# A recurrence chain and its group norm: both heads in one PSUM bank, the norm by halves of the tokens, Sqrt and reciprocal in place of Ln and Exp

## The chip, the cores and the metric

The kernel runs on one core of one Trainium2 chip. Its time is the device time of one execution, in microseconds. Engine names in the rows: PE is TensorE (PEld its weight loads), DVE is VectorE, ACT is ScalarE, POOL is GpSimd, SP is SyncE, which issues the DMAs.

## The reference

256 tokens pass two blocks of width 2048 in float32. The first block has two layers of windowed attention beside a gated convolution. The second has an RWKV-7 mixer of 16 heads (64 wide) beside latent attention, an output projection and a gated feed-forward part. The change is mostly in what follows the RWKV scan:

```python
y = rwkv7_scan(r, decay, k, v, -kk, kk * a)
mu = jnp.mean(y, axis=-1, keepdims=True)                 # over the 64 of a head
var = jnp.mean(jnp.square(y - mu), axis=-1, keepdims=True)
y = ((y - mu) * lax.rsqrt(var + GN_EPS)).reshape(bsz, s, c) * gn_w + gn_b
bonus = jnp.sum(r * k * r_k, axis=-1, keepdims=True) * v
out = (y + bonus.reshape(bsz, s, c)) * g                 # g = sigmoid(h_g) @ g2
x = x + jnp.concatenate([out, y_mla], axis=-1) @ w_out
```

## The kernel before

Weights come in 385 MB of "units", each 128 x 2048 floats, that pass a ring of four places. SyncE loads unit u + 4 when TensorE has finished unit u (`sp_unit`); ScalarE copies it rounded (`act_split`, L229), VectorE or GpSimd subtracts to get the low part (L234, L241), and TensorE multiplies: per block k of the operand one matmul of 128x512 with the high part (L259; the last one L262) and one of 128x256 with the low part (L260), in `both_halves`. Every engine runs its list of stages in the order in which they are written; only semaphores tie the engines together.

**The front** (`phase_front`, once for each of two layers) goes through positions m = 0 to 45, a unit each. Beside the units it does the attention of head pair h: scores on TensorE, softmax, `transposes(h)` at m = 12 + 4h into PSUM banks 2 and 3, `probs(h)` on ScalarE (L585, the copy of them into SBUF), and `values(h)` on TensorE (L885) at m = 13 + 4h. On ScalarE `probs(h)` stands at m = 13 + 4h, behind the split of that position. From m = 36 on, ScalarE has a `gate(m)` (L563) at the end of each position that waits for VectorE.

**Within** (`phase_within`): 16 items (8 pairs of heads, two halves of the tokens). In it TensorE computes for chunks of 32 tokens what the recurrence needs.

**The chain** (`phase_chain`): 8 chunks, c = 1 to 7 in sequence. TensorE computes "next" (L2072, the next state, 16 products of 64x64 tiles) and "y" (L2074, 16 products), one tile for each of the two heads of a pair: rows 0 to 63 and rows 64 to 127. Head 0 writes bank 2 (or 4), head 1 bank 3 (or 5). VectorE adds step_n to each half (L2092) and y to kk (L2099). Between chunks TensorE does something else: `early_products` of the first units of the output projection out2 (which need only the attention half of the operand) and `gates(x)` (L2056 with 128 rows and L2057 with 32 rows), which ScalarE (L2043) and VectorE (L2105) read.

**The norm** (`phase_norm`): `head_sums` (L1713) of y over the heads, VectorE subtracts the mean (L2161), ScalarE squares (L2145), head sums of the squares, ScalarE Ln (L2148) and Exp with -0.5 (L2151), VectorE multiplies and adds (L2165, L2172, L2173), ScalarE and VectorE write the high (L2154) and low (L2169) part of the operand, two blocks at a time. Here a "half" is four of the eight blocks of channels with all tokens.

**out2** (`phase_residual` with `early`): units 0 to 3 were loaded and split long before, and blocks 8 to 15 of each are already multiplied; blocks 0 to 7 of unit 0 wait for the norm's operand pair by pair. `keep_running` (L298) issues matmuls of 128x512 whose result nobody reads ("fillers"): 8 at the end of within, 4 and 2 in the norm, 9 between the blocks of unit 0. Two more pairs of them lie in the last item of within and stay.

`link(...)` makes VectorE wait for its own previous instruction.

## Time and profile before

| | |
|---|---|
| Time, median of 3 runs | 2209.92 us (2209.63 to 2210.14) |
| The profiled execution: its time, its span | 2208.75 us, 2207.0 us |
| Mean granted TensorE clock | 0.998 |
| TensorE busy | 2169.7 us, 98% of the span |
| VectorE, ScalarE, GpSimd busy | 1713.8, 1071.9 and 544.9 us |
| Moved by DMA | 384.73 MB, 174 GB/s |

The span is from the first to the last record of the profiled execution; its time is what the same execution took by the measure of the runs, 1.75 us more. A granted clock of 1.00 is the full one (2.4 GHz), 0.50 the half (1.2 GHz). Busy times are those of an engine's instructions; matmuls overlap in the records, so that a busy TensorE needn't be at its peak.

### The profile page before, as it was taken

What the parts mean: (1) busy time and instruction counts of PE and PEld (TensorE: products, weight loads), DVE (VectorE), ACT (ScalarE), POOL (GpSimd) and SP (SyncE); (2) the same over time, 40 slices, a digit from 0 to 9 for tenths busy, and PEclk for the clock granted to TensorE, in tenths of its full rate; (3) what the DMA queues carried; (4) which work ended last, traced back from release to release, by engine and by line L of the source; (5) the groups of instructions that cost most, each with busy time, mean ns of one, the idle gap of its engine ahead of it and who ended that gap; (6) DMA issues with size and microseconds to landing.
All of it is one profiled execution on the core that took longest, in us unless ns stands there. A gap on an engine that the chain in (4) does not pass through costs nothing.

```text
span 2207.0 us, 38356 instructions
## 1 busy us (share of the span) xinstructions
PE 2169.7 (98%) x14358; PEld 1893.7 (86%) x14358; DVE 1713.8 (78%) x2889; ACT 1071.9 (49%) x1435; POOL 544.9 (25%) x225
## 2 busy tenths in 40 slices
PE   7999999999999999999999999999999999999997
PEld 6888888888888888899999787888888888888886
DVE  7799678886999588788888666888888874447887
ACT  5555464444555654556545533444444443333454
POOL 4776731018776620210003302100000000000001
PEclk9999999999999999999999999999999999999999
DMA  7554445555555455554455200555555555555554
GB/s 256 186 180 174 159 173 190 190 181 202 183 175 181 153 182 182 189 193 166 156 180 181 82 22 26 204 189 184 183 187 189 190 190 185 184 185 189 190 212 169
DMA packets 69030, 384.73 MB, mean 174 GB/s; under 512 B 15088, under 2 KB 22768, under 8 KB 23984
## 3 DMA queue, kind: packets, MB, share of 16 engines
q1 hardware_dynamic: 68912, 383.09, 48.9%
q8 instruction: 82, 1.34, 0.3%
q14 instruction: 36, 0.29, 0.0%
HBM read 379.89 MB, written 3.18 MB: 174 GB/s over the span
## 4 chain that ended last, share of the span: by engine, by line
PE 68%; POOL 14%; issue 11%; DVE 4%; DMA 1%; ACT 1%; SPq 0%; POOLq 0%; DVEq 0%; ACTq 0%
PE ps L259 33%; PE ps L260 18%; POOL low L241 14%; PE ps L247 3%; PE ps L248 3%; PE ps L249 3%; PE ps L262 2%; DMA raw<-weights_dram 1%; DVE low L234 1%; PE ps L1861 1%; PE ps L1913 0%; PE ps L1905 0%; PE ps L1713 0%; PE ps L1850 0%; DMA inst<-chunk_mats_dram 0%
## 5 line engine op out<-in xcount | busy, mean ns | idle before, releaser
L259 PE MATMUL ps<-opA,whi 128*128 128x512 f32 x2460 | 871.2, 394 | 0.0
L260 PE MATMUL ps<-opA,low 128*128 128x256 f32 x2624 | 706.7, 279 | 0.2 <-DVE opA L983 0.2
L229 ACT ACTIVATE whi<-raw 128x2048 fp32r<-128x2048 f32 x346 | 660.2, 1909 | 78.5 <-DMA raw<-weights_dram 77.2
L234 DVE TENSOR_TENSOR low<-raw,whi 128x2048 fp32r<-128x2048 f32 x252 | 583.9, 2317 | 67.0 <-ACT whi L229 51.1
L259 PEld LDWEIGHTS ps<-opA,whi 128*128 128x128 f32 x2460 | 461.0, 187 | 106.0 <-issue 3.0
L241 POOL TENSOR_TENSOR low<-raw,whi 128x2048 fp32r<-128x2048 f32 x95 | 436.4, 4610 | 409.0 <-ACT whi L229 382.7
L259 PE MATMUL ps<-opB,whi 128*128 128x512 f32 x1380 | 494.1, 398 | 14.0 <-DVE opB L418 11.6
L260 PEld LDWEIGHTS ps<-opA,low 128*128 128x128 f32 x2624 | 492.0, 187 | 14.6 <-DVE opA L983 0.5
L260 PE MATMUL ps<-opB,low 128*128 128x256 f32 x1472 | 397.5, 280 | 0.0
L259 PEld LDWEIGHTS ps<-opB,whi 128*128 128x128 f32 x1380 | 259.7, 188 | 77.5 <-DVE low L412 10.4
L268 ACT ACTIVATE crossed<-ps 128x256 f32<-128x256 f32 x168 | 64.5, 384 | 492.0 <-PE ps L262 491.8
L260 PEld LDWEIGHTS ps<-opB,low 128*128 128x128 f32 x1472 | 277.3, 188 | 7.7
L723 DVE SCALAR_TENSOR_TENSOR ps<-a_in,par,ps 128x256 f32<-128x256 f32 x464 | 226.8, 489 | 14.6
L259 PE MATMUL ps<-act_hl,whi 128*128 128x512 f32 x672 | 237.2, 394 | 0.3
L1126 POOL MEMSET ssq<- 128x256 f32 (+1 forms) x4 | 1.5, 367 | 805.0 <-DVE t L975 677.2
L260 PE MATMUL ps<-act_hl,low 128*128 128x256 f32 x704 | 191.4, 279 | 0.0
L247 PE MATMUL ps<-opB,whi 128*128 128x256 f32 x560 | 161.2, 288 | 0.2 <-DVE ps L1435 0.2
L249 PE MATMUL ps<-opB,low 128*128 128x256 f32 x560 | 158.0, 282 | 0.0
L248 PE MATMUL ps<-opB,whi 128*128 128x256 f32 x560 | 157.7, 282 | 0.0
L259 PEld LDWEIGHTS ps<-act_hl,whi 128*128 128x128 f32 x672 | 125.9, 187 | 30.9 <-issue 2.2
L260 PEld LDWEIGHTS ps<-act_hl,low 128*128 128x128 f32 x704 | 132.0, 187 | 2.6
L1130 POOL TENSOR_TENSOR ssq<-ssq,sq 128x256 f32<-128x256 f32 (+1 forms) x63 | 60.6, 962 | 249.2 <-ACT sq L1043 184.3
(393 smaller groups left out, 2608.7 us busy)
## 6 DMA issues: line engine op xcount, KB each, us to landing
raw<-weights_dram SPq DMA_DIRECT2D x350, 1024.0 KB, 4.8
bias_t<-table_dram SPq DMA_DIRECT2D x16, 384.0 KB, 5.9
hT<-xT_dram SPq DMA_DIRECT2D x4, 512.0 KB, 9.0
out_dram<-hT SPq DMA_DIRECT2D x3, 512.0 KB, 2.8
lora_g<-lora_dram SPq DMA_DIRECT2D x1, 1024.0 KB, 5.1
p_in<-pT_dram SPq DMA_DIRECT2D x2, 256.0 KB, 5.1
lora_wa<-lora_dram SPq DMA_DIRECT2D x1, 512.0 KB, 6.4
chunk_mats_dram<-compact SPq DMA_DIRECT2D x4, 128.0 KB, 3.3
```

What stands on the lines that cost most here:

```text
L229: act.activation(whi[:, v % RING, :], raw[:, v % RING, :], ACT.Copy).then_inc(hi_done.sem, 1)
L234: v_.tensor_tensor(wlo(v % RING, 0, width), raw[:, v % RING, 0:width], whi[:, v % RING, 0:width].bitcast(F32), ALU.subtract).then_inc(lo_d ...
L241: pool.tensor_tensor(wlo(v % RING), raw[:, v % RING, :], whi[:, v % RING, :].bitcast(F32), ALU.subtract).then_inc(lo_done.sem, 1)
L247: pe.matmul(dst, whi[:, s, w0:w0 + P], op[:, k, 0:T], start=start, stop=False)
L248: pe.matmul(dst, whi[:, s, w0:w0 + P], op[:, k, T:2 * T], start=False, stop=False)
L249: return pe.matmul(dst, wlo(s, w0, w0 + P), op[:, k, 0:T], start=False, stop=stop)
L259: pe.matmul(*cross, start=start, stop=False)
L260: mm = pe.matmul(ps[:, b, 0:T], wlo(s, w0, w0 + P), op[:, k, 0:T], start=False, stop=False)
L262: mm = pe.matmul(*cross, start=False, stop=True)
L268: act.activation(crossed[:, b, :], ps[:, b if bank is None else bank, T:2 * T], ACT.Copy).then_inc(read.sem, 1)
L723: link(v.scalar_tensor_tensor(y, taps, w, y, ALU.mult, ALU.add))
L1130: pool.tensor_tensor(total, total, part, ALU.add).then_inc(summed.sem, 1)
```

## The change

Five things, in the words of the code:

- **Front.** `probs(h)` for h = 0 to 6 stands on ScalarE at m = 12 + 4h, after the copy of that position's half and before `gate(m)`, instead of behind the split of the next position. `probs(7)` stays.
- **Chain, heads in one bank.** Both heads' "next" go to bank 2, both "y" to bank 4; VectorE adds all 128 partitions in one instruction.
- **Gates in one tile shape.** The second product of a gate takes all 128 rows (the added rows of the weights are zero); gates come after chunks 1, 2, 3 and 5.
- **Norm by halves of the tokens.** A "half" is now 128 tokens of all eight blocks. The first half's tokens are finished after chunk 3: its head sums (kk after chunk 4, squares after chunk 6), its centring, squares, Sqrt and first multiplication move into the chain. Ln and Exp give way to Sqrt on ScalarE and a reciprocal on VectorE.
- **Order and fillers.** Early products: unit 0 before the chain, unit 1 after chunk 7, units 2 and 3 in the norm, blocks 8 to 11 of all four behind the last head sums. ScalarE's copy and GpSimd's subtraction of y_mla's second half move into within; scm, held and the bank of unit 0 move. The fillers at the end of within, in the norm and in unit 0 are left out.

The core of the diff (context and smaller lines left out):

```diff
-if x == 0 and 1 <= h <= PAIRS:
+if x == 0 and h == PAIRS:
...
+if x == 3 and 0 <= h < PAIRS - 1:
+    probs(h)
...
-pe_unit(pe, u0, j, i, op, kb=KB // 2, start=False, bank=early[m], need=0, ready=ready if opening else None, wide=True,
-        filler=(lambda k: (3 if k in (2, 4, 6) else 0, 2)) if opening else None)
+pe_unit(pe, u0, j, i, op, kb=KB // 2, start=False, bank=early[m], need=0, ready=ready if opening else None, wide=True)
...
-def head_sums(pe, src, half):
-    for n in range(4 * half, 4 * half + 4):
-        mm = pe.matmul(ps[:, 2 + n // 2, (n % 2) * T:(n % 2) * T + T], head_ones[:, :], src[:, n, :], start=True, stop=True)
+def half(x, h):
+    return x[:, :, h * P:h * P + P]
+def head_sums(pe, src, h):
+    for b in range(2):
+        mm = pe.matmul(ps[:, 5 + b, :], head_ones[:, :], src[:, 4 * b:4 * b + 4, h * P:h * P + P], start=True, stop=True)
-sums = ps[:, 2:6, :].rearrange("p b (c t) -> p (b c) t", c=2)
+sums = ps[:, 5:7, :].rearrange("p b (c t) -> p (b c) t", c=4)
+sq_, rstd = uS[:, 0:8, :], uS[:, 16:24, :]
+def centred(v, h):
+    v.wait_ge(*rw_p(2 * h + 1))
+    v.scalar_tensor_tensor(half(kk, h), sums, -1.0 / DH, half(kk, h), ALU.mult, ALU.add).then_inc(no["centred"].sem, 1)
...
-scm = place("scm", [P, 2, 2, 3, P], at=second + 24 * T)
-def phase_within(u_next):
+scm = place("scm", [P, 2, 2, 3, P], at=word_rows)
+def phase_within(u_next, op):
...
+pool.wait_ge(*ch["mla_hi"](1))
+pool.tensor_tensor(op[:, 12:16, T:2 * T], y_mla[:, 4:8, :], op[:, 12:16, 0:T].bitcast(F32), ALU.subtract).then_inc(ch["mla_lo"].sem, 1)
...
-keep_running(pe, u_next, 8, 2)
...
+if n == 4:
+    act.wait_ge(*ml["stored"](MLA_H))
+    act.activation(op[:, 12:16, 0:T], y_mla[:, 4:8, :], ACT.Copy).then_inc(ch["mla_hi"].sem, 1)
...
-held = place("held", [P, 4, DH], at=word_rows)
+held = place("held", [P, 4, DH], at=word_rows + 6 * T)
...
-early_bank = (6, 7, 0, 1)
+early_bank = (3, 7, 0, 1)
-        both_halves(pe, u, early_bank[n], k * P, op, k, k == (8 if n >= 2 else 12), False)
+        both_halves(pe, u, early_bank[n], k * P, op, k, k == 12, False)
...
-pool.wait_ge(*ch["state"](1))
-pool.wait_ge(*ch["mla_hi"](1))
-pool.tensor_tensor(op[:, 12:16, T:2 * T], y_mla[:, 4:8, :], op[:, 12:16, 0:T].bitcast(F32), ALU.subtract).then_inc(ch["mla_lo"].sem, 1)
...
-act.wait_ge(*wi["mn"](4 * RW_B))
-act.activation(op[:, 12:16, 0:T], y_mla[:, 4:8, :], ACT.Copy).then_inc(ch["mla_hi"].sem, 1)
+act.activation(small[:, 3:4], small[:, 7:8], ACT.Sqrt)
-        act.wait_ge(*ch["state"](NCH - 1))
-        act.activation(op[:, 8:12, 0:T], y_mla[:, 0:4, :], ACT.Copy).then_inc(ch["mla_hi"].sem, 1)
+        act.wait_ge(*no["centred"](1))
+        act.activation(half(sq_, 0), half(kk, 0), ACT.Square).then_inc(no["sq"].sem, 1)
+act.wait_ge(*ch["state"](NCH - 1))
+act.activation(op[:, 8:12, 0:T], y_mla[:, 0:4, :], ACT.Copy).then_inc(ch["mla_hi"].sem, 1)
+act.wait_ge(*rw_p(2))
+act.activation(half(rstd, 0), sums, ACT.Sqrt, scale=1.0 / DH, bias=small[:, 6:7]).then_inc(no["dev"].sem, 1)
...
-        mm = pe.matmul(dst, lora_g[0:32, 1, n * P:n * P + P], g1[0:32, :], start=False, stop=True)
+        mm = pe.matmul(dst, lora_g[:, 1, n * P:n * P + P], g1, start=False, stop=True)
+pe.wait_ge(*ch["mla_lo"](1))
+early_products(pe, u_next, 0, range(12, 16), op)
...
-                        mm = pe.matmul(ps[r, 2 + h, pair * DH:pair * DH + DH], step_m[r, pair, c // 4, c % 4, :], s, start=True, stop=True)
+                        mm = pe.matmul(ps[r, 2, pair * DH:pair * DH + DH], step_m[r, pair, c // 4, c % 4, :], s, start=True, stop=True)
-                        mm = pe.matmul(ps[r, 4 + h, pair * CH:pair * CH + CH], s, r_[r, pair, c * CH:c * CH + CH], start=True, stop=True)
+                        mm = pe.matmul(ps[r, 4, pair * CH:pair * CH + CH], s, r_[r, pair, c * CH:c * CH + CH], start=True, stop=True)
-        if c == 1:
-            pe.wait_ge(*ch["mla_lo"](1))
-        if c <= 2:
-            early_products(pe, u_next, c - 1, range(12, 16), op)
-        elif c <= 6:
-            gates(c - 3)
+        if c <= 3:
+            gates(c - 1)
+        elif c == 4:
+            pe.wait_ge(*ch["y_read"](3))
+            head_sums(pe, kk, 0)
+        elif c == 5:
+            gates(3)
+        elif c == 6:
+            pe.wait_ge(*no["sq"](1))
+            head_sums(pe, sq_, 0)
+        else:
+            early_products(pe, u_next, 1, range(12, 16), op)
+    link = dve_chain.start(v)
-            for h in range(2):
-                r = slice(DH * h, DH * h + DH)
-                ins = v.tensor_tensor(state[r, (c + 1) % 2, :, :], ps[r, 2 + h, :].rearrange("p (b d) -> p b d", b=RW_B),
-                                      step_n[r, :, c // 4, c % 4, :], ALU.add)
-            ins.then_inc(ch["state"].sem, 1)
+            v.tensor_tensor(state[:, (c + 1) % 2, :, :], ps[:, 2, :].rearrange("p (b d) -> p b d", b=RW_B),
+                            step_n[:, :, c // 4, c % 4, :], ALU.add).then_inc(ch["state"].sem, 1)
-        for h in range(2):
-            r = slice(DH * h, DH * h + DH)
-            dst = kk[r, :, c * CH:c * CH + CH]
-            ins = v.tensor_tensor(dst, ps[r, 4 + h, 0:T].rearrange("p (b t) -> p b t", b=RW_B), dst, ALU.add)
-        ins.then_inc(ch["y_read"].sem, 1)
-        if c >= 4:
-            x = c - 4
+        dst = kk[:, :, c * CH:c * CH + CH]
+        v.tensor_tensor(dst, ps[:, 4, 0:T].rearrange("p (b t) -> p b t", b=RW_B), dst, ALU.add).then_inc(ch["y_read"].sem, 1)
+        if c in (2, 3, 4, 6):
+            x = min(c - 2, 3)
+        if c == 4:
+            centred(v, 0)
+        if c == 6:
+            v.wait_ge(*no["centred"](1))
+            link(v.tensor_tensor(half(gate_w, 0), half(gate_w, 0), half(kk, 0), ALU.mult))
+    link.end()
-y, sq_, rstd = kk, uS[:, 0:8, :], uS[:, 16:24, :]
-def half(x, h):
-    return x[:, 4 * h:4 * h + 4, :]
-    keep_running(pe, u_next, 4, 2)
-    for h in range(2):
-        head_sums(pe, y, h)
-    pe.wait_ge(*ch["mla_lo"](2))
-    early_products(pe, u_next, 0, range(8, 10), op)
-    for h in range(2):
-        pe.wait_ge(*no["sq"](h + 1))
-        head_sums(pe, sq_, h)
-    early_products(pe, u_next, 0, range(10, 12), op)
-    early_products(pe, u_next, 1, range(8, 12), op)
+    pe.wait_ge(*no["dev"](1))
+    head_sums(pe, kk, 1)
-        early_products(pe, u_next, n, range(8, 16), op)
-    pe.wait_ge(*no["ln"](2))
-    keep_running(pe, u_next, 2, 2)
+        early_products(pe, u_next, n, range(12, 16), op)
+    pe.wait_ge(*no["sq"](2))
+    head_sums(pe, sq_, 1)
+    pe.wait_ge(*ch["mla_lo"](2))
+    for n in range(4):
+        early_products(pe, u_next, n, range(8, 12), op)
-    act.activation(small[:, 3:4], small[:, 7:8], ACT.Ln)
-    for h in range(2):
-        act.wait_ge(*no["centred"](h + 1))
-        act.activation(half(sq_, h), half(y, h), ACT.Square).then_inc(no["sq"].sem, 1)
-    for h in range(2):
-        act.wait_ge(*rw_p(h + 3))
-        act.activation(half(rstd, h), half(sums, h), ACT.Ln, scale=1.0 / DH, bias=small[:, 6:7]).then_inc(no["ln"].sem, 1)
-    for h in range(2):
-        act.wait_ge(*no["ln"](h + 1))
-        act.activation(half(rstd, h), half(rstd, h), ACT.Exp, scale=-0.5).then_inc(no["rstd"].sem, 1)
+    act.wait_ge(*no["centred"](2))
+    act.activation(half(sq_, 1), half(kk, 1), ACT.Square).then_inc(no["sq"].sem, 1)
+    act.wait_ge(*rw_p(4))
+    act.activation(half(rstd, 1), sums, ACT.Sqrt, scale=1.0 / DH, bias=small[:, 6:7]).then_inc(no["dev"].sem, 1)
...
-for h in range(2):
-    v.wait_ge(*rw_p(h + 1))
-    v.scalar_tensor_tensor(half(y, h), half(sums, h), -1.0 / DH, half(y, h), ALU.mult, ALU.add).then_inc(no["centred"].sem, 1)
-v.wait_ge(*ch["g_read"](RW_B // 2))
+v.wait_ge(*no["dev"](1))
+link(v.reciprocal(half(rstd, 0), half(rstd, 0)))
+centred(v, 1)
+link(v.tensor_tensor(half(gate_w, 0), half(gate_w, 0), half(rstd, 0), ALU.mult))
+link(v.tensor_tensor(half(gate_w, 0), half(gate_w, 0), half(bonus, 0), ALU.add))
-for h in range(2):
-    link(v.tensor_tensor(half(gate_w, h), half(y, h), half(gate_w, h), ALU.mult))
+link(v.tensor_tensor(half(gate_w, 1), half(gate_w, 1), half(kk, 1), ALU.mult))
+v.wait_ge(*no["dev"](2))
+link(v.reciprocal(half(rstd, 1), half(rstd, 1)))
-    v.wait_ge(*no["rstd"](n // 2 + 1))
-    link(v.tensor_tensor(pair_of(gate_w, n), pair_of(gate_w, n), pair_of(rstd, n), ALU.mult))
-    v.tensor_tensor(pair_of(gate_w, n), pair_of(gate_w, n), pair_of(bonus, n), ALU.add).then_inc(no["gated"].sem, 1)
+    last = half(pair_of(gate_w, n), 1)
+    link(v.tensor_tensor(last, last, half(pair_of(rstd, n), 1), ALU.mult))
+    v.tensor_tensor(last, last, half(pair_of(bonus, n), 1), ALU.add).then_inc(no["gated"].sem, 1)
...
```

## Rows read from the trace of the kernel before

**Rows 1.** Busy by stretch: length; PE, PEld, DVE, ACT, POOL; granted clock; DMA.
```profile
1351.00:1369.00 18.00, 18.00 (x113) 15.28 (x110) 11.06 (x15) 10.96 (x13) 1.24 (x1) 1.00 0.00 1
```

**Rows 2.** The chain of work that ended last, steps 6, 7 and norm: start, us, what.
```profile
1346.20 1.08 PE ps L2072 x32
1347.28 0.91 PE ps L2074 x32
1348.18 0.63 PE ps L2056 x2
1348.81 0.62 PE ps L2057 x2
...
1350.69 1.05 PE ps L2074 x32
...
1352.87 3.55 PE ps L1713 x16
```

**Rows 3.** Timeline of VectorE, chain and norm: start, us, engine, line, operation, [idle before].
```profile
1325.63 1.39 DVE L2092 TENSOR_TENSOR state<-ps,step_n 64x512 f32<-64x512 f32 x2 [1.25 <-PE ps L2072]
...
1351.79 0.86 DVE L2099 TENSOR_TENSOR kk<-ps,kk 64x256 f32<-64x256 f32 x2 [1.28 <-PE ps L2074]
...
1357.79 2.49 DVE L2165 TENSOR_TENSOR gate_w<-kk,gate_w 128x1024 f32<-128x1024 f32 x2
...
1370.99 1.47 DVE L2169 TENSOR_TENSOR opB<-gate_w,opB 128x512 fp32r<-128x512 f32 x2
```

**Rows 4.** Timeline of TensorE: first chain step, ends of units 0 and 1, start of unit 4.
```profile
1324.44 1.15 PE L2072 MATMUL ps<-state,step_m 64*64 64x64 f32 x32 [0.19 <-DVE state L2086]
...
1373.69 0.39 PE L262 MATMUL ps<-opB,whi 128*128 128x512 f32 x1
...
1376.50 0.40 PE L262 MATMUL ps<-opB,whi 128*128 128x512 f32 x1
...
1383.94 0.47 PE L259 MATMUL ps<-opB,whi 128*128 128x512 f32 x1 [1.44 <-DVE small L1093]
```

**Rows 5.** Timeline of ScalarE: within stage (the first row) and norm.
```profile
1314.93 0.28 ACT L1964 ACTIVATE tokA<-ps 128x128 f32<-128x128 f32 x1 [2.04 <-PE ps L1905]
...
1355.99 1.06 ACT L2145 ACTIVATE uS<-kk 128x1024 f32<-128x1024 f32 x1 [2.91 <-DVE kk L2161]
...
1360.86 1.12 ACT L2148 ACTIVATE uS<-ps,small 128x1024 f32<-128x1024 f32 x1 [0.62 <-PE ps L1713]
```

**Rows 6.** Reciprocals, grouped by line and shape: count, busy us, mean ns, idle before.
```profile
L448 DVE RECIPROCAL rs<-sq 128x256 f32<-128x256 f32 x1 | 1.8, 1753 | 0.1
L1809 DVE RECIPROCAL st<-st 128x2 f32<-128x2 f32 x8 | 1.3, 158 | 0.1
```

**Rows 7.** Waits of TensorE over the whole kernel: us in total, times, longest.
```profile
PE ps L885 <- ACT probsT L585: 2.8, 2, 1.4
```

**Rows 8.** Timeline of ScalarE around position 37 of the first front.
```profile
249.75 0.39 ACT L563 ACTIVATE ps<-az 128x256 f32<-128x256 f32 x1 [4.58 <-DVE bz_s L711]
...
251.88 1.00 ACT L585 ACTIVATE probsT<-ps 128x1024 f32<-128x1024 f32 x1
```

**Rows 9.** Timeline of TensorE at the same place.
```profile
244.77 0.71 PE L876 MATMUL ps<-ident,sm 128*128 128x128 f32 x5
...
252.93 1.08 PE L885 MATMUL ps<-probsT,v_tok 128*64 128x256 f32 x8 [1.41 <-ACT probsT L585]
```

**Rows 10.** Busy time and granted clock at the kernel's end (columns as in rows 1).
```profile
2194.00:2196.00 2.00, 0.52 (x3) 0.27 (x2) 1.20 (x4) 0.66 (x2) 0.00 (x0) 1.00 0.00 0
2196.00:2198.00 2.00, 0.43 (x2) 0.03 (x1) 0.95 (x1) 0.47 (x1) 0.00 (x0) 0.81 0.00 0
```

**Rows 11.** Timeline of TensorE, early matmuls of the kernel.
```profile
11.17 0.63 PE L259 MATMUL ps<-opB,whi 128*128 128x512 f32 x1
...
11.81 0.63 PE L259 MATMUL ps<-opB,whi 128*128 128x512 f32 x1
...
17.55 0.44 PE L259 MATMUL ps<-opB,whi 128*128 128x512 f32 x1
```

More of the change, by code:

```diff
@@ L495, in reuse_front_semaphores @@
                                    (ch, ("state", "next", "y", "y_read", "mla_hi", "mla_lo", "g", "g_read", "shift")),
-                                   (no, ("lora", "centred", "sq", "var", "ln", "rstd", "gated", "hi", "lo"))):
+                                   (no, ("lora", "centred", "sq", "dev", "gated", "hi", "lo"))):
                 for n in names:
@@ L2300, in program @@
         u += IN2_UNITS + UP_UNITS
-        following = phase_within(u)
+        following = phase_within(u, opnd[1])
         stages += [phase_mla(u, following), following]
```

## The prediction, made before the changed kernel was run

> **What bounds the kernel now.** I read the busy time by stretches first: in the norm stage TensorE is busy for all 18 us, at the full clock, and VectorE for 11 of them [rows 1]. But part of that TensorE work are fillers, so the chain of waits comes next. In a chain step with gates it runs over TensorE alone: the "next" products 1.08 us, the "y" products 0.91, then four gate products of 0.62 to 0.63 us each, 4.5 us a step [rows 2]. VectorE's timeline shows the other loop: two state additions 1.39 us, two y additions 0.86 [rows 3]. The norm that follows is a dependence chain over three engines. TensorE's timeline shows where it ends: unit 0 of out2 is done at 1374.08, and unit 4 starts at 1383.94, 9.9 us later, after 1.44 us of waiting [rows 4]. Unit 4's weights are only loaded when unit 0 is done, while units 1 to 3 take 8.4 us (2.81 each [rows 4]): so the end of unit 0 sets the end of the kernel, and some 1.4 us of TensorE's work in units 1 to 3 is free. In the front I read the list of waits, then both timelines: values() waits twice for probsT, 1.4 us each time [rows 7].
>
> **The front.** The wait is at position 37, one in each layer. probs(6) stands behind gate(36), which ScalarE gets to at 249.75 only (it waits for VectorE), and behind the split at 250.07; it runs at 251.88, and TensorE resumes at 252.93 with 1.41 us idle. The transposes that probs(6) reads began at 244.77 [rows 8, 9]. Moved ahead of gate(36), it runs near 246 and the wait is gone. Behind it: the gate and the split stay where VectorE puts them, and I see nothing that the chain would meet later that isn't itself released by TensorE. At the six earlier positions the copy now delays a weight split by about 1.1 us; GpSimd, whose subtraction uses that split, is still busy with the previous one then, so I take 0. Term: 2 x 1.41 = -2.8 us. Bounds: 0 and -2.8.
>
> **End of the within stage.** The 8 fillers give way to four early products of unit 0 (4 x 0.35 = 1.4 us). Both lie beside the last evictions; "next" still waits for VectorE's first state copy, so its start at 1324.44 stays. ScalarE's copy of y_mla (128x1024, about 1.06 us as Square over as many elements) moves to item 4; ScalarE has some 2 us idle in each item [rows 5]. Without that cover it would cost 1 us. GpSimd's subtraction goes with it; GpSimd has nothing to do there. 0.
>
> **The chain.** Two halves of 64 partitions become one instruction of 128: state 1.39 to 0.70 us, y 0.86 to 0.43 [rows 3]. The loop over VectorE is then 1.15 + 0.7 + 0.45, under TensorE's step, so this is worth only 0.43 us, at the last y. The gates: each of their products takes two matmul records of 256 columns. The head sums of the same size run at 3.55/16 = 0.22 to 0.23 us a record, 0.46 a product, against 0.62 and 0.63 here, where products with 128 rows and with 32 alternate [rows 2]. I take the difference, 0.16 us, for the change of shape. In one shape only the first pays it: 0.63 + 3 x 0.465 = 2.02 us instead of 2.5. (If it is something else, the gates stay at 2.5: four steps x 0.48 = +1.9 us.) The two head sums that move in are 16 records' worth halved, 1.86 + 0.16 = 2.02 us too. Steps 1 to 6 each hold such a filler: 6 x (1.08 + 0.91 + 2.02) = 24.06 us, then y 1.05 and the addition 0.43. From 1324.44 that ends at 1349.98; before it was 1351.79 + 0.86 = 1352.65. Term -2.7. The waits that come in (gate weights read, shift, centred, square) I placed on this grid; each is satisfied 0.5 us or more before TensorE asks. Of ScalarE's work there, two splits, the Sqrt table load and the first gate read end near 1330, and VectorE needs that read at 1331.
>
> Heads in one bank could cost. The two halves are row tiles 0 to 63 and 64 to 127, which today write two banks and overlap: 32 records of 64 columns in 1.08 us are 0.034 each, while 256 columns of a full tile at 0.23 are 0.058 for 64 [rows 2]. Without the overlap, "next" takes 32 x 0.058 = 1.86 us, +0.78 in six steps = +4.7 us; "y", with 32 columns, stays where it is. Every pair of row tiles in this kernel writes two banks, so no row here shows the case. The Trainium skill (TensorEngine Tiling, "Gotcha 1: PSUM Pressure") says that different row tiles cannot access the same PSUM bank simultaneously; by it the 4.7 us would be paid. I take 0, because the two halves also differ in their output partitions, and keep it as a rival.
>
> **The norm.** Ln and Exp on ScalarE go; Sqrt and VectorE's reciprocal over 128x1024, twice, come. The rows for reciprocals: 128x2 0.158 us, 128x256 1.753 us, so 1.595/254 = 6.28 ns an element [rows 6]; a tensor_tensor over 128x1024 at 1.25 us is some 1.2 ns an element [rows 3]. Over 1024 elements: 0.158 + 1022 x 0.00628 = 6.58 us each. Bounds: from below 1.75, if the cost went by instruction (the 2-element row speaks against that); from above 4 x 1.753 = 7.0. The Trainium skill (VectorE: DVE Perf Modes, "First, the fixed hardware budget") gives the iterative divide a repeat count of 8; at eight passes of about 1.04 ns an element, an estimate, each would be 8.5 us and the sum 3.9 us more. The rows decide for 6.58.
>
> VectorE from 1350.0: reciprocal(0) 6.58 (its Sqrt, as long as today's Ln, 1.12 us [rows 5], ends at 1349.6), centred(1) 1.25, times rstd, plus bonus, times kk: 3 x 1.25 [rows 3]. Meanwhile centred(1) releases Square 1.06, head sums 1.86 and Sqrt 1.12 [rows 5], 4.2 us with hand-overs, so dev(2) comes at 1362.15, 0.5 us after VectorE is free. Then reciprocal(1) to 1368.8, and the tail (eight 128x256 operations at 0.43, and low parts at 0.7 which wait for ScalarE's high parts) 6.0 us: the last low part ends at 1374.85, against 1372.46 before [rows 3]. The 9 + 4 + 2 fillers go. From the last low part to unit 0's end it was 1374.08 - 1372.46 = 1.62 us, three fillers among them, so about 0.95 now (k 6, k 7 at 0.35 and the drain). Unit 0 ends at 1375.8 instead of 1374.08: +1.7 us for chain and norm together, the chain's -2.7, the norm's +5.1 and -0.7 for the fillers.
>
> **The clock.** TensorE now has two gaps: about 1355.8 to 1359.0, and 1366.6 to 1371.2, after which pairs of products come one per 1.3 us. What gaps do shows at the end of the kernel: with 0.52 us of work in 2 us and then 0.43, the granted clock, 1.00 until 2196, has a mean of 0.81 over 2196 to 2198: at half from near 2197.2 on, some 3 us after dense work ended [rows 10]. The kernel's first products take 0.64 us per k (11.17 to 11.81), where 0.35 (2.81/8) is normal; at 17.55 the same matmul takes 0.44 us instead of 0.63 [rows 4, 11], so the slow pace lasted up to 6 us. I expect the fall to 1.2 GHz in the second gap: unit 0's last pair 1.3 us later, and of the slow start in units 1 to 3 (up to 5 k x 0.29 = 1.5 us) most is covered by the free 1.4: +0.3. Term +1.6.
>
> **Sum.** -2.8 + 1.7 + 1.6 = +0.5 us. The profiled execution took 2208.75 us (span 2207.0), so 2209.3 on it; the median of the runs is 2209.92, 1.2 higher: **2210.4 us**.
>
> **Rivals.**
> - The clock holds in both gaps: 2210.4 - 1.6 = 2208.8. For it: TensorE is not quite empty in between. Chance 0.22.
> - It falls in the first gap too: the head sums of the second half take 1.9 us more, on the path: 2212.3. The gap is 3.2 us, at the length that the kernel's end shows. 0.14.
> - The front's wait moves elsewhere (the y_sq sums at 39, where TensorE already waits now and then): 2213.2. 0.10.
> - Slower: row tiles in one bank don't overlap, +4.7: 2215.1. It decides (past 2214.3) once "next" takes over 1.73 us, 0.65 more in six steps. For it: the kernel gives every other pair of row tiles two banks; against it: here their output partitions differ. 0.10. The gates' shape not being the cause (+1.9: 2212.3): 0.05.
> - The change does more than this: reciprocals by instruction, not by element. Then centred, Square, sums and Sqrt bind, and unit 0 ends 8 us earlier: 2202. 0.03.
> - My forecast, a fall in the second gap only: 0.36, with its own range 2208 to 2212.
>
> **Range and chances.** 0.2% is 4.4 us, about what a measurement of this kernel can tell from no change. Faster than 2205.5 lies only the cheap reciprocal and an error in my grid: 0.06. Slower than 2214.3: the bank rival, or two of the +2 cases together: 0.14. Same: 0.80. The range 2206 to 2214.5 leaves out the bank rival and the cheap reciprocal.
>
> **What would show it.** Reciprocals of 6.6 us at the two new lines; "next" at 1.1 us; steps of 4.0 us; no wait of values() at position 37; granted clock under 1.00 in the stretch behind the norm; unit 0 of out2 done 51 to 53 us after the first "next" begins (49.64 before). The forecast is wrong if "next" takes 1.8 us, if a reciprocal is far from 6.6 us, or if the clock stays low through units 1 to 3 of out2.

## The result, and the profile after

The changed kernel takes 2213.49 us (median of 20 executions, 2210.35 to 2215.34), the kernel before 2209.4 us in the same measurement (20 executions, 2208.08 to 2210.55). The ratio is 1.0017, with a 95% interval of 1.0011 to 1.0024: slower by 3.8 us by the ratio and by 4.1 us by the medians. That is under the 0.2% that I took as the limit, though the interval reaches past it. The profiled executions say nearly the same: a span of 2210.3 us against 2207.0, +3.3. One of the twelve executions of e1 below took 2352.9 us at a mean granted clock of 0.849, where all others here have 0.994 or more; the ratios leave it out.

| us | before | after | forecast for after |
|---|---|---|---|
| span of the profiled execution | 2207.0 | 2210.3 | 2207.5 |
| first "next" begins | 1324.44 | 1321.59 | 1321.6 |
| from there until y of chunk 7 is added | 28.21 | 26.48 | 25.54 |
| until the last low part is written | 48.02 | 52.53 | 50.4 |
| until unit 0 of out2 is done | 49.64 | 53.59 | 52.7 |
| from there until unit 4 starts | 9.86 | 10.60 | 10.2 |
| unit 4, first to last record | 5.88 | 7.38 | 5.9 |

The four stretches that add up to the end are the second, fifth, sixth and seventh row: -2.85 + 3.95 + 0.74 + 1.50 = +3.3 us, the whole difference of the spans. What follows shows the rows behind them.

**The front.** Two timelines of the kernel after around position 37, ScalarE and then TensorE. The copy of the probabilities stands at 245.68, behind the transposes, and `values()` starts as unit 36 ends, with no wait ([rows 8, 9] had 251.88 and 1.41 us idle). In the list of TensorE's waits it no longer appears ([rows 7]).

```profile
245.68 1.03 ACT L585 ACTIVATE probsT<-ps 128x1024 f32<-128x1024 f32 x1 [0.35 <-PE ps L878]
...
251.29 0.40 PE L262 MATMUL ps<-opB,whi 128*128 128x512 f32 x1
251.61 1.08 PE L887 MATMUL ps<-probsT,v_tok 128*64 128x256 f32 x8
```

**A chain step.** The timeline of TensorE, kernel after, first step: "next", "y", one gate pair by pair, and the next "next". Compare [rows 2] and the first of [rows 4].

```profile
1321.59 1.15 PE L2088 MATMUL ps<-state,step_m 64*64 64x64 f32 x32 [0.62 <-DVE state L2108]
1322.57 1.07 PE L2090 MATMUL ps<-uS,state 64*64 64x32 f32 x32
1323.58 0.70 PE L2070 MATMUL ps<-uS,lora_g 128*128 128x256 f32 x2
1324.11 0.59 PE L2071 MATMUL ps<-uS,lora_g 128*128 128x256 f32 x2
1324.54 0.59 PE L2070 MATMUL ps<-uS,lora_g 128*128 128x256 f32 x2
1324.97 0.59 PE L2071 MATMUL ps<-uS,lora_g 128*128 128x256 f32 x2
1325.50 1.15 PE L2088 MATMUL ps<-state,step_m 64*64 64x64 f32 x32
```

A record's length overlaps the next one, so read the starts. "next" holds TensorE for 0.98 us, with both heads in one bank; the first and the last gate product for 0.53, the two between them for 0.43. The step is 3.91 us, and all six (1321.59, 1325.50 and so on to 1345.03, the last "y") are alike.

**The end of the chain and the norm.** The timeline of VectorE, kernel after, with GpSimd's one record of this stretch (POOL) in its place by time; compare [rows 3].

```profile
1344.18 2.36 POOL L2040 TENSOR_TENSOR opB<-y_mla,opB 128x1024 fp32r<-128x1024 f32 x1 [12.20 <-ACT opB L2056]
1344.35 3.27 DVE L2128 TENSOR_TENSOR gate_w<-gate_w,kk 128x1024 f32<-128x1024 f32 x1
1347.65 0.42 DVE L2117 TENSOR_TENSOR kk<-ps,kk 128x256 f32<-128x256 f32 x1
1347.99 6.54 DVE L2168 RECIPROCAL uS<-uS 128x1024 f32<-128x1024 f32 x1
1354.57 1.22 DVE L1724 SCALAR_TENSOR_TENSOR kk<-ps,kk 128x1024 f32<-128x1024 f32 x1
...
1358.22 1.23 DVE L2173 TENSOR_TENSOR gate_w<-gate_w,kk 128x1024 f32<-128x1024 f32 x1
1361.67 6.55 DVE L2179 RECIPROCAL uS<-uS 128x1024 f32<-128x1024 f32 x1 [2.23 <-ACT uS L2159]
...
1372.65 1.47 DVE L2177 TENSOR_TENSOR opB<-gate_w,opB 128x512 fp32r<-128x512 f32 x2
```

Three things are to be seen. The reciprocals take 6.54 and 6.55 us. The multiplication at 1344.35 takes 3.27 us, where the four operations of its size in the norm take 1.22 to 1.23; it lies beside GpSimd's subtraction, and VectorE isn't free for the last y (whose products were done at 1346.15) until 1347.65. And before the second reciprocal VectorE idles for 2.23 us, which ScalarE's Sqrt ends; the Sqrt waits for head sums (TensorE's timeline below).

GpSimd's subtraction follows ScalarE's copy of y_mla's first half, and that copy follows the last state addition in both kernels (done at 1348.72 before and at 1343.01 after). The timelines of ScalarE and GpSimd, kernel before:

```profile
1348.75 1.06 ACT L2040 ACTIVATE opB<-y_mla 128x1024 fp32r<-128x1024 f32 x1 [1.67 <-DVE state L2092]
1349.88 2.36 POOL L2029 TENSOR_TENSOR opB<-y_mla,opB 128x1024 fp32r<-128x1024 f32 x1 [13.50 <-ACT opB L2040]
```

and ScalarE's, kernel after:

```profile
1343.05 1.06 ACT L2056 ACTIVATE opB<-y_mla 128x1024 fp32r<-128x1024 f32 x1 [0.97 <-DVE state L2113]
```

TensorE's timeline, kernel after, with the head sums, the two gaps and the ends of the units:

```profile
1348.13 1.98 PE L1717 MATMUL ps<-kk,head_ones 128*128 128x512 f32 x4 [0.38 <-DVE kk L2117]
...
1356.93 3.49 PE L1717 MATMUL ps<-uS,head_ones 128*128 128x512 f32 x4 [4.02 <-ACT uS L2157]
...
1370.69 0.76 PE L259 MATMUL ps<-opB,whi 128*128 128x512 f32 x1 [4.67 <-DVE opB L2177]
...
1374.78 0.40 PE L262 MATMUL ps<-opB,whi 128*128 128x512 f32 x1
...
1385.78 0.47 PE L259 MATMUL ps<-opB,whi 128*128 128x512 f32 x1 [2.18 <-DVE small L1095]
```

The same four head-sum matmuls take 1.98 us at 1348.13 and 3.49 behind 4.02 us of idle time. The windows of the kernel after say why (columns as in [rows 1]; the granted clock is the number behind ACT's and POOL's):

```profile
1356.00:1358.00 2.00, 1.06 (x2) 0.55 (x3) 1.97 (x2) 0.88 (x1) 0.00 (x0) 0.64 0.00 0
1358.00:1360.00 2.00, 2.00 (x5) 0.96 (x3) 1.41 (x2) 0.00 (x0) 0.00 (x0) 0.50 0.00 0
...
1370.00:1372.00 2.00, 1.31 (x4) 1.05 (x5) 1.97 (x5) 1.24 (x2) 0.00 (x0) 0.56 0.00 0
...
1386.00:1388.00 2.00, 2.00 (x11) 1.73 (x11) 1.93 (x4) 1.93 (x2) 0.98 (x1) 0.82 0.94 393
1388.00:1390.00 2.00, 2.00 (x8) 1.71 (x7) 2.00 (x2) 0.29 (x1) 0.00 (x0) 0.50 0.00 0
```

The clock fell to half at each of the two gaps, and a third time in unit 4, where TensorE had idled for only 2.18 us. There it fell late: a mean of 0.82 over 1386 to 1388 is half from about 1387.3 on, 1.5 us after TensorE had started again. Between the three stretches it was 1.00. In the kernel before it is 1.00 in every window from 1340 to 1400.

The wait between unit 0 and unit 4 is the load of unit 4's weights. The chain of waits, kernel before:

```profile
1374.27 4.80 DMA raw<-weights_dram
```

and kernel after:

```profile
1375.35 5.55 DMA raw<-weights_dram
```

The split and the subtraction behind it are the same in both (1.93 and 2.29 us). The 0.75 us are the load's.

### The profile page after: what moved, and what is told of

Same layout as the page of the kernel before. It is cut to its first block, busy times and chain, and to the rows that moved or that the text cites. A ratio compares the mean times of both kernels' runs of the same rounds, so it can differ in the third digit from the quotient of the medians.

```text
span 2210.3 us, 38267 instructions
## 1 busy us (share of the span) xinstructions
PE 2166.3 (98%) x14319; PEld 1890.2 (86%) x14319; DVE 1722.0 (78%) x2880; ACT 1069.0 (48%) x1431; POOL 544.3 (25%) x225
## 4 chain that ended last, share of the span: by engine, by line
PE 69%; POOL 15%; issue 10%; DVE 3%; ACT 1%; DMA 1%; SPq 0%; POOLq 0%; DVEq 0%; ACTq 0%
PE ps L259 33%; PE ps L260 18%; POOL low L241 14%; PE ps L247 3%; PE ps L249 3%; PE ps L248 3%; PE ps L262 2%; DMA raw<-weights_dram 1%; PE ps L1871 1%; PE ps L1925 0%; PE ps L1917 0%; ACT whi L229 0%; PE ps L1860 0%; DVE uS L2179 0%; PE ps L2088 0%
```

## The experiments

Each kernel ran beside the kernel before on the same chip (medians of the latter: 2209.66 us beside e1 to e4, 2209.14 beside e5 to e8; each ratio is to its own). "Start" is when the first "next" begins in the profiled execution; the three columns behind it are lengths in the same execution.

| kernel | median, us | ratio to before (95%) | start | start to unit 0 done | unit 0 done to unit 4's start | load of unit 4 |
|---|---|---|---|---|---|---|
| before | 2209.4 | | 1324.44 | 49.64 | 9.86 | 4.80 |
| after | 2213.49 | 1.0017 (1.0011 to 1.0024) | 1321.59 | 53.59 | 10.60 | 5.55 |
| e1, front only | 2206.85 | 0.9987 (0.9978 to 0.9996) | 1322.89 | 49.65 | 9.88 | 4.83 |
| e2, all but the front | 2215.61 | 1.0029 (1.0018 to 1.0039) | 1325.26 | 54.75 | 10.57 | 5.52 |
| e3, fillers back | 2211.10 | 1.0007 (0.9998 to 1.0016) | 1321.21 | 52.73 | 10.63 | 5.58 |
| e4, GpSimd later | 2211.67 | 1.0010 (1.0001 to 1.0018) | 1323.94 | 52.52 | 10.57 | 5.53 |
| e5, Ln and Exp | 2202.47 | 0.9968 (0.9956 to 0.9981) | 1322.39 | 43.57 | 12.52 | 7.49 |
| e6, gates with 32 rows | 2215.01 | 1.0028 (1.0018 to 1.0039) | 1320.99 | 57.33 | 10.72 | 5.67 |
| e7, Ln and Exp, reordered | 2201.70 | 0.9964 (0.9950 to 0.9978) | 1322.60 | 42.78 | 10.17 | 5.13 |
| e8, VectorE in halves | 2213.36 | 1.0019 (1.0010 to 1.0028) | 1322.24 | 55.14 | 10.05 | 5.00 |

The start scatters: among the eight kernels with the new front it lies between 1320.99 and 1323.94, though only e1 differs in what comes ahead of it. So the stretches from the start on are compared one by one, and the start only as a mean.

**e1_front_only.** The kernel before with the edit of the front alone:

```diff
-if x == 0 and 1 <= h <= PAIRS:
+if x == 0 and h == PAIRS:
     probs(h - 1)
...
+if x == 3 and 0 <= h < PAIRS - 1:
+    probs(h)
 if m in GATED:
```

> The kernel before with the front's edit alone (probs(h) ahead of the gate). My theory: the 1.41 us wait of values() at position 37 goes in both layers and nothing takes its place, so 2.8 us less than before (2209.4 to 2206.6). Rival: the chain stage of the changed kernel starts 2.85 us earlier for another reason (the shorter end of within), and the front gives nothing: no change.

Measured: 0.9987, which is 2.8 us less by the medians (0.9 to 4.9 by the interval). The clock stays at 1.00 through chain and norm, and the stretches behind the start are those of the kernel before to 0.03 us. In the list of TensorE's waits the two for probsT are gone (2.8 us in all before), and the wait on the y_sq sums, where the rival of the prediction would have them go, is what it was (0.5 us in two waits):

```profile
PE ps L894 <- ACT y_sq L649: 0.5, 2, 0.3
```

What follows: the front gives what its two waits held, and the wait didn't go elsewhere. How near the 2.8 us are to the forecast is partly luck, since the interval is wide, and in the profiled executions the chain starts only 1.55 us earlier.

**e2_no_front.** The changed kernel with the front as before (the reverse of the edit above).

> The changed kernel with the front's edit undone, so chain and norm alone. My theory: the front hides 2.8 us of what chain and norm cost; they alone are 6.2 to 6.9 us slower than before (2215.6 to 2216.3). Rival, the front gives nothing: 3.3 to 4.1 us slower, as the changed kernel.

Measured: 1.0029, 6.4 us above the kernel before (4.0 to 8.6 by the interval) and 2.1 us above the changed kernel by the medians. That fits the theory; the rival's 3.3 to 4.1 lies at the edge of the interval. Together with e1: the mean start with the new front is 1322.2 (eight profiles), without it 1324.85 (two), 2.6 us apart. In this execution the clock fell in the same two gaps, but the second time it stayed at half almost to the end of unit 0 at 1380.01 (the windows from 1374 to 1378 show 0.50, the one from 1378 to 1380 shows 0.61): counted from the start, unit 0 is done 1.2 us later than in the changed kernel. TensorE's timeline of e2:

```profile
1360.60 3.78 PE L1715 MATMUL ps<-uS,head_ones 128*128 128x512 f32 x4 [4.02 <-ACT uS L2155]
...
1374.65 0.77 PE L259 MATMUL ps<-opB,whi 128*128 128x512 f32 x1 [3.91 <-DVE opB L2175]
```

**e3_fillers_back.** Fillers where the changed kernel has its gaps:

```diff
+keep_running(pe, u_next, 14, 2)
 pe.wait_ge(*no["sq"](2))
 head_sums(pe, sq_, 1)
...
 for n in range(4):
     early_products(pe, u_next, n, range(8, 12), op)
+keep_running(pe, u_next, 16, 2)
...
 pe_unit(pe, u0, j, i, op, ..., wide=True,
+        filler=(lambda k: (3 if k in (2, 4, 6) else 0, 2)) if opening else None)
```

> The changed kernel with fillers in TensorE's two gaps of the norm (14 ahead of the last head sums, 16 behind the last early products) and the 3 + 3 + 3 between the blocks of unit 0. My theory: the granted clock holds at 1.00, the last head sums take 2.0 us instead of 3.5, unit 0 and unit 4 run at full pace; 3 to 3.5 us less than the changed kernel, so 2210. Rival: VectorE's reciprocals set the end of the norm whatever the clock does, and the low clock is hidden: no more than 1 us less than the changed kernel.

Measured: 1.0007, 2.4 us below the changed kernel by the medians; the theory had 3 to 3.5, the rival 1 at most. The timeline of TensorE, and of VectorE where the reciprocal stands:

```profile
1356.55 1.98 PE L1718 MATMUL ps<-uS,head_ones 128*128 128x512 f32 x4 [0.82 <-ACT uS L2160]
...
1359.79 6.56 DVE L2182 RECIPROCAL uS<-uS 128x1024 f32<-128x1024 f32 x1 [0.73 <-ACT uS L2162]
...
1368.81 0.47 PE L259 MATMUL ps<-opB,whi 128*128 128x512 f32 x1 [1.04 <-DVE opB L2180]
```

The gaps shrink to 0.82 and 1.04 us, the granted clock is 1.00 in every window from 1356 to 1390, the head sums are back at 1.98, and VectorE waits 0.73 us for the Sqrt instead of 2.23. The low clock is worth the 1.5 us at the head sums, and by the profiles another 1.5 in unit 4. Of the 1.5 us, 0.6 goes again in unit 0: from the last low part to its end it takes 1.69 us with the fillers and 1.06 in the changed kernel. That 0.6 is what the theory left out.

**e4_pool_later.** GpSimd's subtraction waits for the last y:

```diff
+pool.wait_ge(*ch["y_read"](NCH - 1))
 pool.wait_ge(*ch["mla_hi"](2))
```

> The changed kernel, GpSimd's subtraction of y_mla's first half waits for the last y addition, so that it no longer runs beside VectorE's multiplication of gate_w by kk (128x1024), which took 3.27 us where the same shape takes 1.23. My theory: the two engines slow each other when both read SBUF; the multiplication takes 1.23 us, the last y addition and the first reciprocal start 1.5 us earlier, and the kernel is 1.5 us faster than the changed one (2212.0). Rival: the 3.27 us are a wait inside that instruction for something else (the gate read), and stay; no change against the changed kernel. If the subtraction now slows the reciprocal beside it, that one is longer than 6.54 us.

Measured: 1.0010, 1.8 us below the changed kernel by the medians; their intervals overlap, so the timing alone doesn't settle it. The timeline of VectorE and GpSimd does:

```profile
1346.71 1.22 DVE L2129 TENSOR_TENSOR gate_w<-gate_w,kk 128x1024 f32<-128x1024 f32 x1
1348.62 0.42 DVE L2118 TENSOR_TENSOR kk<-ps,kk 128x256 f32<-128x256 f32 x1 [0.69 <-PE ps L2091]
1348.96 6.54 DVE L2169 RECIPROCAL uS<-uS 128x1024 f32<-128x1024 f32 x1
1349.12 2.37 POOL L2041 TENSOR_TENSOR opB<-y_mla,opB 128x1024 fp32r<-128x1024 f32 x1 [14.81 <-DVE kk L2118]
```

The multiplication is back at 1.22 us, and the reciprocal starts 25.02 us after the start instead of 26.40. Beside the reciprocal, GpSimd's subtraction lengthens nothing: e7 has the same subtraction while VectorE is idle, at 2.38 us, and the second reciprocal, with GpSimd idle, takes 6.55.

**e5_ln_exp.** The changed kernel with Ln and Exp on ScalarE in place of Sqrt and the reciprocals:

```diff
-act.activation(half(rstd, h), sums, ACT.Sqrt, scale=1.0 / DH, bias=small[:, 6:7]).then_inc(no["dev"].sem, 1)
+act.activation(half(rstd, h), sums, ACT.Ln, scale=1.0 / DH, bias=small[:, 6:7]).then_inc(no["dev"].sem, 1)
+act.wait_ge(*no["dev"](h + 1))
+act.activation(half(rstd, h), half(rstd, h), ACT.Exp, scale=-0.5).then_inc(no["rstd"].sem, 1)
...
-v.wait_ge(*no["dev"](h + 1))
-link(v.reciprocal(half(rstd, h), half(rstd, h)))
+v.wait_ge(*no["rstd"](h + 1))
```

(`centred(v, 1)` stands ahead of the first of these waits, and the table is loaded ahead for Ln.)

> The changed kernel with Ln and Exp on ScalarE for both halves, as in the kernel before, in place of Sqrt and VectorE's two reciprocals of 6.54 us; the Ln table is loaded ahead of each Ln. My theory: the reciprocals are the whole loss. The second half's Exp ends near 1358, ten us before the second reciprocal did (1368.2), TensorE has no gap over 2 us left and keeps its clock: 9 to 11 us less than the changed kernel, 6 to 7 less than before (2202.5 to 2203.5). Rival: the table loads (1.28 us each) and ScalarE's order eat it, since ScalarE does splits, Ln and Exp in one queue: 4 us or less gained against the changed kernel (2209.5).

Measured: 0.9968, 11.0 us below the changed kernel by the medians and 6.7 below the kernel before. ScalarE's timeline:

```profile
1355.48 1.12 ACT L2162 ACTIVATE uS<-ps,small 128x1024 f32<-128x1024 f32 x1 [2.21 <-PE ps L1717]
1356.61 1.28 ACT L2164 ACT_TABLE_LOAD   x1
1357.90 1.06 ACT L2164 ACTIVATE uS<-uS 128x1024 f32<-128x1024 f32 x1
```

Exp costs 2.4 us behind Ln, its table load included, where the reciprocal cost 6.55 behind the Sqrt; and the first half's pair, 6.54 us on VectorE, now lies on ScalarE behind the chain. Unit 0 is done 10.0 us sooner, with waits of at most 0.45 us between its pairs. But the kernel doesn't get all of it in this profile: unit 4's load takes 7.49 us, so TensorE idles for 4.11 us, which the theory didn't expect, and the clock is at half soon after unit 4 has started (a mean of 0.81 over 1378 to 1380). TensorE's timeline and the windows of e5:

```profile
1378.48 0.48 PE L259 MATMUL ps<-opB,whi 128*128 128x512 f32 x1 [4.11 <-DVE small L1095]
...
1380.00:1382.00 2.00, 2.00 (x8) 1.71 (x8) 2.00 (x1) 1.00 (x1) 0.25 (x1) 0.50 0.03 12
```

**e6_gates_32_rows.** The gates' second product with 32 rows again:

```diff
-mm = pe.matmul(dst, lora_g[:, 1, n * P:n * P + P], g1, start=False, stop=True)
+mm = pe.matmul(dst, lora_g[0:32, 1, n * P:n * P + P], g1[0:32, :], start=False, stop=True)
```

> The changed kernel with the gates' second product again over 32 rows. My theory: each alternation of the tile's shape costs 0.16 us or a little more, a gate step is 4.4 to 4.5 us instead of 3.91, four such steps: 2.0 to 2.3 us slower than the changed kernel (2215.6). Rival: the 0.62 us came from something else and the step stays at 3.91: no change against the changed kernel.

Measured: 1.0028, 1.5 us above the changed kernel by the medians. TensorE's timeline:

```profile
1322.98 0.70 PE L2070 MATMUL ps<-uS,lora_g 128*128 128x256 f32 x2
1323.61 0.69 PE L2071 MATMUL ps<-uS,lora_g 32*128 32x256 f32 x2
1324.23 0.70 PE L2070 MATMUL ps<-uS,lora_g 128*128 128x256 f32 x2
1324.86 0.69 PE L2071 MATMUL ps<-uS,lora_g 32*128 32x256 f32 x2
1325.49 1.15 PE L2088 MATMUL ps<-state,step_m 64*64 64x64 f32 x32
```

Every product now holds TensorE for 0.63 us, and the step has 4.50 us instead of 3.91. A gate step of the changed kernel has two changes of shape, at its two ends (64x64 tiles to 128x128 and back); this one has five. So 0.59 us go to three more changes, 0.2 us each. The last y is added 28.81 us after the start instead of 26.48, 2.33 later, which is four steps of 0.58. (That unit 0 ends 3.7 us later, and not 2.3, is the clock: here it was at half up to unit 0's last matmul, which is 1.1 us more behind the last low part, and the last head sums took 3.78 us, 0.3 more.) By the timing alone the theory (2.0 to 2.3 us) can't be told from less, as the intervals of the two kernels overlap; the step in the trace decides.

**e7_ln_exp_order.** e5 with e4's wait and with unit 3's early products behind the last head sums:

```diff
+pool.wait_ge(*ch["y_read"](NCH - 1))
...
-for n in (2, 3):
+for n in (2,):
     early_products(pe, u_next, n, range(12, 16), op)
 pe.wait_ge(*no["sq"](2))
 head_sums(pe, sq_, 1)
+early_products(pe, u_next, 3, range(12, 16), op)
```

> The kernel of the run with Ln and Exp, and two orders more: GpSimd's subtraction behind the last y addition, and unit 3's early products behind the last head sums. My theory: another 1 us, 2201.5 to 2202.5; the last chunk's addition is no longer late and the last head sums start when the squares are there. Rival: TensorE is the bound by then and its work is the same: no difference from the run with Ln and Exp.

Measured: 0.9964 (0.9950 to 0.9978), which can't be told from e5, so the timing doesn't decide between the theory's 1 us and the rival. In the profile unit 0 is done 0.8 us sooner than in e5, VectorE's multiplication takes 1.22 us again, and the clock is 1.00 in every window from 1346 to 1396. TensorE's timeline:

```profile
1352.88 1.98 PE L1717 MATMUL ps<-uS,head_ones 128*128 128x512 f32 x4 [1.00 <-ACT uS L2163]
...
1375.55 0.48 PE L259 MATMUL ps<-opB,whi 128*128 128x512 f32 x1 [1.76 <-DVE small L1095]
```

**e8_two_halves.** VectorE adds 64 partitions at a time, as before, out of the one bank:

```diff
-v.tensor_tensor(state[:, (c + 1) % 2, :, :], ps[:, 2, :]..., step_n[:, :, c // 4, c % 4, :], ALU.add)
+for h in range(2):
+    r = slice(DH * h, DH * h + DH)
+    ins = v.tensor_tensor(state[r, (c + 1) % 2, :, :], ps[r, 2, :]..., step_n[r, :, c // 4, c % 4, :], ALU.add)
```

and the same for y.

> The changed kernel with VectorE's state and y additions again one for each head (64 partitions), both from the one bank. My theory: TensorE sets the step, so only the last y addition shows, 0.4 us slower than the changed kernel, which a timing can't tell; the step stays at 3.91 us. Rival: one instruction for both heads is what shortened the step, and it grows towards 4.5 us: 3 us slower or more (2216.5).

Measured: 1.0019, the same as the changed kernel. VectorE's timeline:

```profile
1323.44 1.39 DVE L2115 TENSOR_TENSOR state<-ps,step_n 64x512 f32<-64x512 f32 x2 [1.25 <-PE ps L2088]
1324.86 0.86 DVE L2122 TENSOR_TENSOR kk<-ps,kk 64x256 f32<-64x256 f32 x2
1327.35 1.39 DVE L2115 TENSOR_TENSOR state<-ps,step_n 64x512 f32<-64x512 f32 x2 [1.63 <-PE ps L2088]
```

The step is still 3.91 us (1323.44 to 1327.35), with 1.63 us of VectorE idle in it: in the chain the shorter additions are worth nothing, as TensorE sets the step. Behind it they are worth more than the 0.4 us that I expected: the last y is added 27.66 us after the start, against 26.48. The longer last addition is 0.44 of these 1.18 us. The other 0.74 come from the last state: it is ready 0.7 us later, ScalarE's copy and GpSimd's subtraction follow it (the latter 23.32 us after the start, against 22.59), and VectorE's multiplication ends behind them as before. In the profile unit 0 is done 1.6 us later than in the changed kernel, and unit 4 gives that back: its load is 0.55 us shorter and its clock doesn't fall.

## Why the prediction was nearly right

The forecast of +0.5 us was 3.6 too low against the medians (3.3 by the ratio, 2.8 by the spans); the time lies inside the range, near its upper end, and within 0.2% of before, as the likeliest class said. It was not the forecast's own case that came true but a rival with company: the fall of the clock in the first gap too. Part of the nearness is luck: misses of 4.4 us stand against 1.5 us by which other terms came out cheaper (the list of terms below). One of the signs that I had named failed by a little: unit 0 was done 53.59 us after the first "next", and I had 51 to 53.

**The front: -2.8 predicted, -2.8 measured** (e1), and the rival that its wait moves elsewhere is refuted by e1's list of waits.

**Heads in one bank.** "next" holds TensorE for 0.98 us in one bank; it is as short as in two (1324.44 to 1325.42 in the kernel before). The 4.7 us of the bank rival are not there. That row tiles 0 to 63 and 64 to 127 overlap when they write different partitions of one bank is what the 32 records in 1.15 us show. (The Trainium skill, TensorEngine Tiling, "Gotcha 1: PSUM Pressure", has it that different row tiles can't access one bank at once; this case's trace doesn't agree for tiles with their own output partitions.)

**The chain: steps of 4.01 predicted, 3.91 measured.** The 0.16 us that I took for the change of shape is 0.2 in e6, and the gates in one shape take 1.92 us instead of 2.02: two of the four products hold TensorE for 0.53 us, not one for 0.63. ("next" and "y" are 0.98 and 1.01 us by their starts, where I had read 1.08 and 0.91 off the chain of waits; the sum is the same.) The rival that the shape is not the cause is refuted. (The Trainium skill, TensorEngine Tiling, "Key Properties", says that a change of tiling mode drains TensorE, with no figure; e6 agrees and gives one.) In sum 0.6 us better than forecast.

**The last y: the step that failed first.** I wrote that each wait coming into the chain is satisfied 0.5 us or more ahead, and priced VectorE's multiplication in it at 1.25 us like its likes. It took 3.27. The reason is a neighbour that I hadn't looked at: the change moves the multiplication into chain step 6, and there it meets GpSimd's subtraction of y_mla's first half, which follows the last state through ScalarE's copy, as it did in the kernel before, and starts at 1344.18. In all six profiles with this overlap VectorE's instruction ends 1.08 or 1.09 us after GpSimd's (1347.62 and 1346.54 here; e2, e3, e5, e6 and e8 likewise). It does so in e8 too (1349.01 and 1347.93), where it began 0.54 us after GpSimd and not 0.17: it is held until the other is through, not slowed in proportion. e4 takes the overlap away and gets 1.4 us back. Beside the reciprocal, which reads one operand and not two, nothing is held. (The Trainium skill, SBUF — State Buffer, "SBUF: two separate sides", describes this: VectorE with two SBUF inputs and GpSimd take turns at a shared port for a whole instruction. The trace agrees, with these numbers; that page was the rule that I should have weighed.) The hold put the last y 1.4 to 1.5 us back; net of the shorter steps it came 0.9 us later than forecast.

**The norm: mis-sized by the head sums.** Both reciprocals are on the forecast, 6.54 and 6.55 us for 6.58. (The repeat count of 8 in the Trainium skill, VectorE: DVE Perf Modes, "First, the fixed hardware budget", read as eight passes, would by estimate have given 8.5; the rows of the reciprocals before were the better guide.) From the last y to the last low part I forecast 24.87 us and it took 26.05: +1.5 us from the head sums at half clock, -0.3 in hand-overs.

**The clock: right in kind, wrong in place.** I expected a fall in the second gap only, +1.3 us in unit 0 and +0.3 behind it. The gaps were 4.02 us (3.2 expected) and 4.67 (4.6), and both made it fall. The first cost 1.5 us (3.49 us instead of 1.98), as the rival with 0.14 said (1.9). The second cost nothing in this execution, as it was over at about 1373.6, ahead of the last pair: unit 0 ended 1.06 us behind the last low part, where I had 2.25. In e2 and e6 it lasted almost or wholly through unit 0, and from the last low part to unit 0's end it took 1.93 and 2.18 us, near the 2.25. So the forecast's 1.3 us is a matter of when the clock rises again. The third fall, in unit 4, cost 1.5 us; I didn't foresee it. Of the seven other profiles with the new chain only e5 has a fall there, behind a wait of 4.11 us; in e2, e3, e4 and e6 the wait is 2.14 to 2.29 us and the clock stays. Those 1.5 us belong to this execution and not surely to the kernel's median. But the median has no less of the low clock: the mean granted clock was 0.996 in the profiled execution and 0.994 in 13 of the 20, and these 13 took 2214.2 us in the mean, where the five with 0.996 took 2211.9. With the fillers of e3 it was 0.997 or 0.998 each time. Where in the program the others lost it no trace shows.

**Unit 4's load: +0.74 us, not foreseen, and open.** It took 4.80 and 4.83 us in the two kernels with the old chain and 5.00 to 7.49 in the eight with the new one, at the same size. No experiment tells what lengthens it.

By terms, against the forecast: last y +0.9, rest of the norm +1.2, end of unit 0 -1.2, units 1 to 3 -0.3, load +0.7, unit 4 at the low clock +1.5: +2.8 us, the difference by the spans.

**Why the whole change doesn't pay** is what e5 shows. With Ln and Exp in their place the same chain, halves and gates make the kernel 6.7 us faster than before, 2.8 of them from the front. The reciprocals take that back: they are 13.1 us of VectorE on the dependence chain, and without them unit 0 is done 10.0 us sooner, the 1.5 us of low clock at the head sums included. Of the other 3.9 us, 2.3 are the gates' shape by e6's profile; no run separates the norm by halves from the rest. The forecast had this price right; it had no reason to ask what the change would be without it. e5 and e7 beat both kernels (0.9968 and 0.9964), and are the versions to keep.

## What to carry to other kernels

When a function moves to another engine, compare the price per element on the dependence chain, with the table load on the other side: here 6.55 us against 2.4. When an edit moves an instruction of VectorE or GpSimd, look at what the other one does at the new place, even if that one isn't touched by the edit: here two operations with both operands in SBUF took turns (3.27 us instead of 1.22), while beside a one-operand instruction like the reciprocal the other was free. A gap on TensorE can cost twice, once itself and once in the dependent matmuls behind it: between 1340 and 1400 in these ten profiles the clock fell at each of the eleven gaps of 3.28 to 4.67 us, for 0 to 1.8 us of the time behind. Fillers in the gap (e3) kept it up.

## What was not expected of the hardware

- VectorE's 128x1024 multiplication held to 3.27 us by GpSimd's 2.36 us subtraction, and always done 1.08 us behind it; the later one loses, and the earlier one isn't lengthened (2.36 against 2.38 alone). It also goes the other way: in the kernel after, GpSimd's 128x256 addition at 1383.50, begun 0.62 us after a VectorE subtraction of two SBUF operands, takes 2.26 us, where the same addition begun first takes 0.74 (1378.79).
- The length of the low-clock stretch behind gaps of about 4 us differs between executions of nearly the same code: in the second gap it ended ahead of the last pair of unit 0 in the changed kernel, and close to or past its end in e2 and e6. A fall after 2.18 us of idle time was seen once; in four other profiles 2.14 to 2.29 us at the same place had none.
- The same 1 MB load behind unit 0 took between 4.80 and 7.49 us over ten profiles. The cause is open.
- The start of the chain, at 1322 us, scatters by 3 us between profiles whose work up to there is the same.
